# Weight tiles 16 bytes off the line, three waits reordered: a four-layer transformer on one core

## What is computed

```python
for layer in range(DEPTH):
    h = modulate(rmsnorm_2(x, norm1_w[layer]), shift1, scale1)
    mix = (pool and chunk attention) if layer % 2 == 0 else mamba2_mixer(h, ...)
    x = x + gate1[:, None, :] * mix
    h2 = modulate(rmsnorm_2(x, norm2_w[layer]), shift2, scale2)
    x = x + gate2[:, None, :] * hier_moe(h2, ...)      # 32 experts, silu(h2 w1) * (h2 w3) @ w2
return rmsnorm_2(x, final_norm_w)
```

## Time and profile before

| | us |
|---|---|
| median of three runs | 2306.08 |
| profiled execution, its own time | 2303.33 |
| its span in the trace | 2301.5 |
| TensorE matmul busy | 2078.0 (90%) |
| TensorE weight load busy | 1971.5 (86%) |
| VectorE busy | 1457.0 (63%) |
| ScalarE busy | 1041.8 (45%) |
| TensorE's granted clock, mean | 0.924 |

### The profile page before, as it was taken

One profiled execution on the slowest core, in us unless ns is written; L12 is line 12 of the kernel. 1 busy time (PEld: TensorE's weight loads), 2 busy tenths in 40 slices (PEclk: granted clock), 3 DMA queues, 4 the chain that ended last, 5 costly groups with the idle time before them and its releaser, 6 DMA issues. The chain is left out here.

```text
span 2301.5 us, 39932 instructions
## 1 busy us (share of the span) xinstructions
PE 2078.0 (90%) x16806; PEld 1971.5 (86%) x16806; DVE 1457.0 (63%) x2365; ACT 1041.8 (45%) x1468; POOL 0.2 (0%) x4
## 2 busy tenths in 40 slices
PE   6978888999989788989998879999979898899997
PEld 6877877999979678779998769999969777899997
DVE  5946555688567655557865666777758655565554
ACT  5643433444465334435444335444455554444443
POOL 0000000000000000000000000000000000000000
PEclk8988888999989888889999889999989988899999
DMA  5322422488543325125975324787724322355552
GB/s 196 121 91 92 156 91 84 143 298 301 185 145 115 98 92 165 65 92 189 323 258 172 126 92 156 269 307 279 280 93 156 123 70 65 126 186 182 181 179 92
DMA packets 101411, 370.15 MB, mean 161 GB/s; under 512 B 11504, under 2 KB 11888, under 8 KB 100976
## 3 DMA queue, kind: packets, MB, share of 16 engines
q1 hardware_dynamic: 99936, 363.38, 47.3%
q10 hardware_dynamic: 1296, 4.21, 0.5%
HBM read 366.50 MB, written 1.05 MB: 160 GB/s over the span
## 5 line engine op out<-in xcount | busy, mean ns | idle before, releaser
L315 DVE TENSOR_TENSOR low<-raw,high 128x1024 fp32r<-128x1024 f32 x590 | 719.2, 1222 | 460.7 <-ACT high L312 458.6
L312 ACT CAST high<-raw 128x1024 fp32r<-128x1024 f32 x590 | 614.0, 1046 | 552.4 <-PE ps L380 487.2
L378 PE MATMUL ps<-hh,high 128*128 128x256 f32 x2832 | 826.8, 292 | 39.3 <-DVE hl L697 28.6
L379 PE MATMUL ps<-hh,low 128*128 128x256 f32 x2832 | 809.6, 286 | 0.0
L380 PE MATMUL ps<-hl,high 128*128 128x256 f32 x2832 | 808.7, 286 | 0.0
L378 PEld LDWEIGHTS ps<-hh,high 128*128 128x128 f32 x2832 | 558.4, 197 | 61.4 <-issue 50.8
L379 PEld LDWEIGHTS ps<-hh,low 128*128 128x128 f32 x2832 | 555.7, 196 | 0.5 <-issue 0.5
L380 PEld LDWEIGHTS ps<-hl,high 128*128 128x128 f32 x2832 | 554.6, 196 | 0.0
L378 PE MATMUL ps<-ffn_high,high 128*128 128x256 f32 x672 | 193.2, 287 | 10.3 <-PEq L1926 5.8
L379 PE MATMUL ps<-ffn_high,low 128*128 128x256 f32 x672 | 190.6, 284 | 0.0
L380 PE MATMUL ps<-ffn_low,high 128*128 128x256 f32 x672 | 190.6, 284 | 0.0
(11 more groups left out here) (450 smaller groups left out, 2777.8 us busy)
## 6 DMA issues: line engine op xcount, KB each, us to landing
raw<-in_stream SPq DMA_DIRECT2D x590, 512.0 KB, 4.0
ada_rows<-in_ada SPq DMA_DIRECT2D x96, 512.0 KB, 5.5
c_act<-in_c SPq DMA_DIRECT2D x3, 512.0 KB, 4.2
bias<-in_bias ACTq DMA_DIRECT2D x1, 1536.0 KB, 7.4
xT<-in_xT SPq DMA_DIRECT2D x4, 256.0 KB, 5.9
out<-xT SPq DMA_DIRECT2D x1, 1024.0 KB, 3.8
par<-in_par ACTq DMA_DIRECT2D x1, 842.0 KB, 9.1
hybrid_const<-in_const ACTq DMA_DIRECT2D x1, 800.0 KB, 6.0
```

Source lines behind the costliest of these rows:

```text
L312: return act.copy(self.high[:, slot, :], self.raw[:, slot, :])
L315: return dve.tensor_tensor(self.low[:, slot, :], self.raw[:, slot, :], self.high[:, slot, :].bitcast(F32), ALU.subtract)
L378: pe.matmul(out, sh, mh, start=start, stop=False, **more)
L379: pe.matmul(out, sl, mh, start=False, stop=False, **more)
```

## The change

It has four parts.

1. **Shift.** `high` and `low` get 64 elements more and are used from element 4 on: every weight block begins 16 bytes later. The moving tensors stay where they were. The larger tensors also move what is allocated behind them: `high` is now used from 144 bytes past a multiple of 1024, `low` from 400 bytes past one; `const`, `par3` and `xT` move as well, and the filler ahead of `hh` takes the difference up, so that `hh` and all behind it stand where they stood.
2. **Sums read sooner.** `keep_sums` moves from VectorE's step j == 3 to step j == 2.
3. **z's first product moved.** It goes from the head of the second Mamba block to the end of the first, with ScalarE's rounding of the unit that follows (`wz.scalar(act, 0)`).
4. **The end of the last mixture by tiles.** The last four experts' down products are made two tiles at a time over all four experts. The additions to `xT`, the squares and their sums (now in bank 2) follow each pair of tiles. The last normalisation stands in the same block, with one dummy ScalarE square root ahead of it, and the result is stored in four transfers of 256 KB.

```diff
+SHIFT = 4
...
-        high = sb("high", [P, RING, UNIT], dt=F32R)
-        low = sb("low", [P, RING, UNIT], dt=F32R)
+        high, low = (sb(n, [P, LINE + RING * UNIT], dt=F32R)[:, SHIFT:SHIFT + RING * UNIT].rearrange("p (s u) -> p s u", s=RING)
+                     for n in ("high", "low"))
...
-        def add_squares(pe, c, turn=0):
+        def add_squares(pe, c, turn=0, bank=4):
 
             pe.wait_ge(squares.sem, squares.base + turn * KD // 2 + c + 1)
             for k in (2 * c, 2 * c + 1):
-                pe.matmul(ps[:, 4, 0:T], ones, sq[:, k, :], start=(k == 0), stop=(k == KD - 1))
+                ins = pe.matmul(ps[:, bank, 0:T], ones, sq[:, k, :], start=(k == 0), stop=(k == KD - 1))
+            return ins
...
-        def rms_norm(gain):
...
-        def mixture(l, norm):
+        def mixture(l, norm, last=False):
...
+            by_tile = range(E_N - RING, E_N) if last else ()
...
+                    if last:
+                        for c in range(KD // 2):
+                            sp.wait_ge(out_scaled.sem, out_scaled.base + c + 1)
+                            sp.dma_start(out[:, 2 * c:2 * c + 2, :], xT[:, 2 * c:2 * c + 2, :]).then_inc(stored, 16)
+                        sp.wait_ge(stored, 16 * KD // 2)
...
-                        if s >= LAG:
+                        if s >= LAG and s - LAG not in by_tile:
                             down(s - LAG)
                             if s < E_N and s % 2:
                                 spread(s // 2)
-                    for c in range(KD // 2):
-                        add_squares(pe, c)
+                    if not last:
+                        for c in range(KD // 2):
+                            add_squares(pe, c)
+                    else:
+                        pe.wait_ge(hidden_done.sem, hidden_done.base + E_N // 2)
+                        for c in range(KD // 2):
+                            for j in by_tile:
+                                halves = w.arrived(pe, down_at(j))
+                                x = (hidh[:, j // 2 % PAIRS, j % 2, :], hidl[:, j // 2 % PAIRS, j % 2, :])
+                                for m in (2 * c, 2 * c + 1):
+                                    ins = three_products(pe, ps[:, 4 + c, m % 2 * T:(m % 2 + 1) * T],
+                                                         [a[:, m * P:(m + 1) * P] for a in halves], x,
+                                                         False, j == E_N - 1, skip_group_check=True)
+                                if c == KD // 2 - 1:
+                                    ins.then_inc(ring.unit_done.sem, 1)
+                            if c < KD // 2 - 1:
+                                tell(ins, tiles_done)
+                            if c:
+                                add_squares(pe, c - 1, bank=2)
+                        tell(add_squares(pe, KD // 2 - 1, bank=2), final_summed)
...
+                    if last:
+                        act.activation(stat[:, 3, 0:1], ones[:, 0:1], ACT.Sqrt)
+                        act.wait_ge(variance.sem, variance.base + 2)
+                        tell(act.activation(stat[:, 1, :], stat[:, 0, :], ACT.Sqrt), deviation)
...
-                    dve.wait_ge(*w.done(3 * E_N - 1))
+                    if not last:
+                        dve.wait_ge(*w.done(3 * E_N - 1))
                     for m in range(KD):
+                        if last and m == KD - 2:
+                            dve.wait_ge(*w.done(3 * E_N - 1))
+                        elif last and m % 2 == 0:
+                            dve.wait_ge(tiles_done.sem, tiles_done.base + m // 2 + 1)
                         ins = dve.scalar_tensor_tensor(xT[:, m, :], ps[:, 4 + m // 2, m % 2 * T:(m % 2 + 1) * T],
                                                        gate_of[:, m:m + 1], xT[:, m, :], ALU.mult, ALU.add)
...
+                    if last:
+                        done = InOrder(dve, dve_step)
+                        dve.wait_ge(final_summed.sem, final_summed.base + 1)
+                        tell(dve.tensor_scalar(stat[:, 0, :], ps[:, 2, 0:T], 1.0 / D, EPS, ALU.mult, ALU.add), variance)
+                        dve.wait_ge(deviation.sem, deviation.base + 2)
+                        done(dve.reciprocal(stat[:, 2, :], stat[:, 1, :]))
+                        for k in range(KD):
+                            ins = dve.scalar_tensor_tensor(xT[:, k, :], xT[:, k, :], P2("final")[:, k:k + 1], stat[:, 2, :],
+                                                           ALU.mult, ALU.mult)
+                            if k % 2:
+                                tell(ins, out_scaled)
...
+                    prod.after_read(pe, max(j for j in range(KX // 2) if prod.pairs[j][0] == prod_z.pairs[0][0]))
+                    for m in range(2):
+                        prod_z.tensor(pe, h, 0, only=m)
...
-                        if j == 3:
+                        if j == 2:
                             keep_sums()
...
+                        if j == KX // 2 - 1:
+                            wz.scalar(act, 0)
...
-                    prod_z.tensor(pe, h, 0, only=0)
-                    prod_z.tensor(pe, h, 0, only=1)
...
-                            wz.scalar(act, 0)
...
-        mixture(1, Norm(mgain[:, 3, :], shift(1, 1), hT))
-        rms_norm(P2("final"))
-        with new_block() as block:
-            @block.sync
-            def _(sp):
-                sp.dma_start(out, xT[:, :, :]).then_inc(stored, 16)
-                sp.wait_ge(stored, 16)
+        mixture(1, Norm(mgain[:, 3, :], shift(1, 1), hT), last=True)
```

15 lines of the change are left out of this document (1 added, 14 removed).

## The result

| | before | after |
|---|---|---|
| median, us (7 runs each) | 2304.03 | 2323.27 |
| ratio to before, 95% interval | | 1.0072 [1.0058, 1.0085] |
| profiled execution, us | 2303.33 | 2321.44 |
| its span, us | 2301.5 | 2319.6 |
| granted clock, mean | 0.924 | 0.934 |

One of the seven executions after took 3029.36 us at a mean granted clock of 0.627; the ratio leaves it out, and the other six lie between 2318.63 and 2323.48.

A forecast was written before the change was run, and what follows sets the result against it. TensorE, busy 90% of the span, was taken as the bound, with dense matmuls at two paces (113.4 and 117.8 ns) plus stops. Forecast: 2306.08 - 12.5 - 29 = 2264.5 us, range 2242 to 2298.

The forecast's parts named there:

- The step: Dense matmul stretches: shifting the weight tiles replaces the 117.8 ns pace by 113.4 over 774 us, winning 29 us.
- the reading behind the step: Dense stretches: weight and moving-tile reads meet in one of two ways, and shifting a start changes how; no separate size.
- the rival: Every dense stretch: the shift hurts, the old 64 bytes being good for the fast pace; 2320 us, chance 0.15.
- Its bound of 24 us: Dense stretches: about 5,500 fast steps turn slow at 4.4 ns each, giving 2317.6 us.
- its further bound of 120 ns: Dense stretches: all 12,048 steps at 120 ns, 2.2 ns more each, 26 us on top.
- Its aside on `low`: Weight tiles: `low` also stands 256 bytes from where it stood against `high`; no separate size.
- the shift does nothing: Dense stretches: read ports are independent, only the phase at a restart sets the pace; 2293.6 us, chance 0.33.
- The rival with 111.6 everywhere: Dense stretches: all steps fall to the weight loads' pace, winning 50 us; 2243.6 us, chance 0.07.
- Sums read sooner: TensorE's stop ahead of the first `turn` shrinks from 7.92 to 2.2 us, winning 5.7 us (5.4 to 7.1).
- z's first product: Turn of the two Mamba blocks: 48 matmuls fill TensorE's 6.33 us idle time, winning 6.3 us (4.5 to 8).
- End by tiles: End of the last mixture: shorter tail against a new TensorE stop of about 3 us; gain 0.5 us (-2 to +2).
- The three together: Waits at first `turn`, Mamba block turn and kernel end: 5.7 + 6.3 + 0.5 = 12.5 us, ends 8 and 17.

The follow-up runs named there:

- the moves alone: The changed kernel with `high` and `low` back at their old places and sizes, the three moves of work kept: 2291.53 us, ratio 0.9946.
- SHIFT = 3: The changed kernel with the weight tiles 12 bytes later instead of 16, 76 bytes from the moving tiles modulo 256: 2278.47 us, ratio 0.9872.
- SHIFT = 61: The changed kernel with the weight tiles 244 bytes later instead of 16, 52 bytes from the moving tiles modulo 256: 2284.81 us, ratio 0.9907.

## Why the prediction was wrong

**The shift, where it failed.** The step was "between 0 and 29 I take 29". It rested on the sight that these matmuls can run at 113.3 for long, and took the slow pace for a disturbance that any shift would break up. What the runs showed in its place: the kernel before already stood at one of the few good distances. Of 64 distances six reach 113.3 and the others lie between 115.5 and 123.3; 64 bytes is one of the six, if one with two paces. Going from 64 to 80 left it for 118.7, and cost 33 us instead of winning 29. That the two streams of reads meet, the reading behind the step, is still not shown: the runs show that the two places count, not what waits for what. Without a row at another distance there was no ground for a sign, and the argument of the rival ("the present 64 bytes were good for it", "slow is what they fall into") read the same rows better. It should have had more than 0.15, as the lot that most places draw. The sentence that "the pace does not change from block to block" holds within a stretch of the trace before, not from one to the next: in the last mixture the 143 matmuls from 2060.1 to 2076.2 ran at 113.5 between neighbours at 117.8, with nothing about their places changed.

**The size of the rival.** It was put at 2320, the result is 2323.3. Its bound of 24 us (4.4 ns on 5,500 steps) was too small, as the new pace is none of the two seen but 118.7 (0.9 ns more on all steps, some 12 us), and its further bound of 120 ns was too large. Measured, the shift costs 33 us by itself. Its aside on `low`, 256 bytes further from `high`, falls: larger tensors without the shift measure 0.9992.

**The rival "the shift does nothing"** falls with the shift alone (1.0144): the same matmuls without any wait on a semaphore take 113.3 to 123.3 ns by where their two operands stand to each other. Its aside on the phase at a restart was half right: at one distance the stretch takes one of two paces at its start and keeps it. The Trainium skill's page "SBUF — State Buffer", section "Who interferes with whom", has the two read ports of TensorE independent and TensorE never waiting; the trace does not agree for this pattern of work, in which the place of the two operands sets the pace, and the measurement decides. 113.3 ns is the least that any run shows with a new weight tile for each 256 columns. The 109.2 ns that the Trainium skill's page "TensorE: Matmul & The Clock Gate", section "Back-to-back issue gap", gives for an isolated pace was reached at none of 64 distances. The rival with 111.6 everywhere falls too.

**Sums read sooner: right in mechanism.** The stop was to shrink to 2.2 us; it is 1.82 (2.09 with the moves alone). I took 5.7 with 7.1 as the upper end "if the clock holds"; it held (1.00 in the windows above), and the lead grew by 7.0.

**z's first product: right, a little high at first.** 6.3 was taken, 4.5 to 8 the bounds; 4.8 is what stands at the start of the heads with the moves alone, and 7.7 in the changed kernel, where the clock did not fall behind the blocks. The stop at the blocks is 0.41 to 0.68 us in these two, as said (under 1), but 2.0 to 2.1 in the five kernels that run at the fast pace ahead of it. I do not count the two stretches of 3.1 us that then went from the heads: other kernels with the same move have them.

**End by tiles: within its bounds, for the reasons named.** Predicted 0.5 with -2 to +2; the traces give +0.5 to -1. The stop of 3 us is there (2.99), the half-clock window behind it too (0.63 from 2260.4 to 2265 with the moves alone), the last store takes 2.5 us from the last scaling where 2.6 was said. What I did not draw from this is that the stop could be had for nothing by starting with the experts whose tiles were ready.

The three together, 12.5 us: measured 13.0 in the medians. That this is so near is in part luck. In the profiled execution the terms are 7.0 + 4.8 - 0.6 = 11.2 us; the two half-clock stretches that happened to be missing gave 6.2, and a somewhat slower mix of the two paces (a mean of 116.00 against 115.72 ns) took 3.6.

## What to carry to other kernels

When a stretch of identical matmuls runs at a pace that changes from stretch to stretch with no wait between, measure the pace against the distance of its two operands in a small kernel first: it costs one run, and here it separated 113.3 from 118.7 ns, 4.8% of each dense step, for 4 bytes. Choose a place at which every kind of restart in the kernel falls into the fast pace, not one at which it can; three stretches for a place were too few to know. And do not count such a gain in full: here 27.5 us of shorter steps came out as 13 in the medians, because the faster engine comes earlier to what it waits for. Do not move what is at a good place by luck on the ground that it might be better elsewhere.

The best version here, weight and moving tiles both 16 bytes later, the moved waits and the last two experts by tiles, takes 2273.1 us against 2304.6, a ratio of 0.9865 [0.9843, 0.9887] to the kernel before, and about 2.1% under the changed one (0.9865 / 1.0072). Its time can't be told apart from that of both sides shifted with four by tiles (2273.8); that two is the better number is read from the trace alone.

## What the runs showed of the hardware that I had not expected

- Back-to-back matmuls with a weight tile each (128 by 128, 256 moving columns, fp32r, clock 1.00) take 113.3 to 123.3 ns, by the distance of weight tile and moving tile modulo 256 bytes, down to steps of 4 bytes (76: 113.3, 80: 118.9, 84: 120.0). Whether the moving tile stands at a multiple of 32 or 16 bytes off it counts as well (80: 118.7 or 119.3; 208: 116.7 or 118.3; 64: two paces or one). Twelve bytes instead of sixteen took the whole kernel from 2323.3 to 2278.5 us.
- At a distance of 64 two paces, 113.3 and 117.8, are each stable until the next interruption: in the kernel before one stretch of 725 matmuls (471.1 to 553.2) holds 113.3 throughout. Other distances have two as well. What interrupts has a part in which it is, and the same stretch of both mixtures mostly took the same one.
- TensorE fell to half clock for stretches worth 3.1 us each while busy all of the time (PE 8.00 of 8.00 us, clock 0.58), in the kernel before, the changed one and those with SHIFT = 3 and with both sides shifted, and in none of the moves alone, SHIFT = 61 and two by tiles, with the same instructions there.
